# Expert weights loaded two units at a time, eight successive rows per partition, in other buffers

## The reference

```python
def expert_block(args):
    tok, gate, e = args
    hid = xt[tok] @ w1[e] + b1[e]
    out = clamped_swiglu(hid) @ w2[e] + b2[e]
    return out * gate[:, None].astype(out.dtype)
...
y = jnp.zeros((n_tok, D), outs.dtype).at[slot_tok].add(outs.reshape(n_pad, D))
```

## Time and profile before

| | |
|---|---|
| median of 3 runs | 1537.73 us (1536.8 to 1537.91) |
| the profiled execution, its own time | 1541.62 us |
| its span, first to last instruction | 1539.9 us |
| mean granted TensorE clock | 0.983 of full speed |
| PE (TensorE) busy | 93% of the span |
| DVE busy | 63% |
| ACT / POOL busy | 17% / 21% |
| queue q1 (loads issued by SP) | 434.49 MB, 71.7% of 16 engines' span |
| queue q0 (issued by POOL) | 20.31 MB, 5.3% |

### The profile page before, as it was taken

The page is one execution under the profiler, slowest core; times in us unless marked ns, Lnnn a source line. Parts: engine busy times, 40 slices in busy tenths (PEclk is TensorE's granted clock), DMA queues, the critical chain, the costliest instruction groups (busy, mean ns, idle before and its releaser), DMA issues.

```text
span 1539.9 us, 31449 instructions
## 1 busy us (share of the span) xinstructions
PE 1437.1 (93%) x12450; PEld 627.7 (41%) x12450; DVE 963.8 (63%) x1821; ACT 256.4 (17%) x461; POOL 317.3 (21%) x428
## 2 busy tenths in 40 slices
PE   9999999898999999999999999999999999999992
PEld 7777878786552233332222222222222222222220
DVE  5499856642446977576665566666556666655664
ACT  4535243320310010001000000100000010000012
POOL 5633551331230001111111111111111111111100
PEclk9999989999999999999999999999999999999996
DMA  5422100130559999999999999999999999999984
GB/s 177 167 78 80 37 17 6 56 110 1 203 216 394 392 402 402 397 392 402 395 396 387 399 384 394 400 393 390 390 395 389 394 396 391 388 394 388 393 333 132
DMA packets 96785, 456.24 MB, mean 296 GB/s; under 512 B 22978, under 2 KB 36968, under 8 KB 47567
## 3 DMA queue, kind: packets, MB, share of 16 engines
q1 hardware_dynamic: 86974, 434.49, 71.7%
q0 software_dynamic: 9600, 20.31, 5.3%
q10 hardware_dynamic: 144, 0.52, 0.1%
HBM read 442.89 MB, written 20.61 MB: 301 GB/s over the span
## 4 chain that ended last, share of the span: by engine, by line
PE 40%; DMA 33%; DVE 12%; SPq 10%; issue 3%; ACT 2%; POOL 0%; DVEq 0%; POOLq 0%; ACTq 0%
DMA slots<-in_expert_w_dram 32%; PE banks L1709 15%; PE banks L1718 8%; SPq L598 6%; PE banks L1651 3%; SPq L603 3%; PE banks L1439 1%; PE banks L1324 1%; PE banks L1325 1%; PE banks L1326 1%; DVE AR L1947 1%; PE banks L1425 1%; PE banks L1536 1%; PE banks L1504 1%; PE banks L1412 1%
## 5 line engine op out<-in xcount | busy, mean ns | idle before, releaser
L1709 PE MATMUL banks<-slots,BK 128*32 128x512 f32 x6144 | 673.6, 594 | 22.6 <-DMA slots<-in_expert_w_dram 21.6
L1709 PEld LDWEIGHTS banks<-slots,BK 128*32 128x32 f32 x6144 | 195.9, 110 | 490.7 <-issue 368.8
L2228 DVE TENSOR_TENSOR qk<-banks,qk 128x1536 f32<-128x1536 f32 x32 | 56.3, 1758 | 276.2 <-PE banks L1709 275.9
L955 POOL DMA_INDIRECT x_sum<-hT,idy x32 | 46.6, 1457 | 675.7 <-issue 577.0
L1718 PE MATMUL banks<-slots,qk 128*32 128x512 f32 x1536 | 172.5, 594 | 13.2 <-DMA slots<-in_expert_w_dram 13.2
L1718 PE MATMUL banks<-slots,hT 128*32 128x512 f32 x1536 | 171.6, 593 | 13.7 <-DMA slots<-in_expert_w_dram 13.0
L2185 DVE STREAM_TRANSPOSE BK<-AR 32x256 f32<-32x256 f32 x384 | 167.0, 435 | 18.8 <-DMA AR<-h_rows,idx 12.8
L1243 ACT ACTIVATE BK<-qk 128x768 f32<-128x768 f32 x32 | 30.5, 952 | 676.9 <-DVE qk L2228 676.9
L1718 PEld LDWEIGHTS banks<-slots,qk 128*32 128x32 f32 x1536 | 47.7, 109 | 135.1 <-issue 93.6
L1718 PEld LDWEIGHTS banks<-slots,hT 128*32 128x32 f32 x1536 | 47.6, 109 | 134.9 <-issue 93.1
L2195 DVE STREAM_TRANSPOSE qk<-AR 32x192 f32<-32x192 f32 x256 | 94.7, 370 | 3.8
(11 more groups left out here) (380 smaller groups left out, 1446.0 us busy)
## 6 DMA issues: line engine op xcount, KB each, us to landing
slots<-in_expert_w_dram SPq DMA_DIRECT2D x384, 1024.0 KB
slots<-in_w_in_dram SPq DMA_DIRECT2D x13, 1024.0 KB, 5.2
xs<-in_x_dram SPq DMA_DIRECT2D x8, 512.0 KB, 5.1
slots<-in_w_out_dram SPq DMA_DIRECT2D x2, 2048.0 KB, 8.7
x_sum<-slots POOLq DMA_DIRECT2D x1, 2560.0 KB
h_rows<-slots SPq DMA_DIRECT2D x4, 512.0 KB, 7.9
slots<-x_sum SPq DMA_DIRECT2D x4, 512.0 KB, 4.8
out_dram<-hT SPq DMA_DIRECT2D x3, 512.0 KB, 2.6
```

Of the source, the lines that this page charges most:

```text
L1709: ins = nc.tensor.matmul(bank[HID + g][j * CB:(j + 1) * CB, :], xT[q][:, k, g * CB:(g + 1) * CB], raw[n % RAW][:, j, :], start=(k == 0), s ...
L2228: tensor_tensor(inner, hid, bias_row.unsqueeze(1).to_broadcast([P, NG, CW]), ALU.add).then_inc(hid_free, 1)
```

## The change

Two neighbouring units become one DMA of 2 MiB with one semaphore and one wait of SP. Partition p now gets rows 8p to 8p + 7 of w1 and of w2: w1's unit k is row 8p + k on partition p, and a pair of units is one run of 16 KiB per partition, with 64 KiB in DRAM from one partition's run to the next (32 KiB for w2). `turn_x`, `x0` and `turn_act` read every eighth element to match; `turn_act` becomes one instruction in place of 16.

Buffers move. The first area of the ring is now `AR`, free before the output projection; `h2row` moves from area 3 to `qk`; `xg`, `act` and `glu_t` move from `AR` to area 0, `g2row` and `squares` to `BK`. With that, SP begins ten units (all 8 of expert 0, 2 of expert 1) before the output projection, 2 more after its last tile, and none after `x0`. The two first bias loads (L608) move behind the wait for the stores and for `xt_full`. The diff, with unchanged lines cut:

```diff
...
         hrow = region(BKf, 0, 2 * D).rearrange("p (b d) -> p b d", b=2)
-        h2row = region(slot_flat[3], 0, TT * D).rearrange("p (t d) -> p t d", t=TT)
+        h2row = region(qkf, 0, TT * D).rearrange("p (t d) -> p t d", t=TT)
         junk = region(ARf, 0, D)
...
         busy = region(ARf, 3 * D, P)
-        squares = region(ARf, D, D)
-        xg = region(ARf, 0, 2 * D).rearrange("p (b d) -> p b d", b=2)
+        squares = region(BKf, 2 * D, D)
+        xg = region(slot_flat[0], 0, 2 * D).rearrange("p (b d) -> p b d", b=2)
+        last_junk = region(slot_flat[0], 0, D)
         def gated(ap):
             return ap.rearrange("p (g f) -> p g f", g=NG)
-        act, glu_t = (gated(region(ARf, n * D, NG * HC)) for n in (2, 3))
+        act, glu_t = (gated(region(slot_flat[0], n * D, NG * HC)) for n in (2, 3))
         lin_t = gated(region(sbf, 0, NG * HC))
-        g2row = region(ARf, 3 * D, D)
+        g2row = region(BKf, 3 * D, D)
         sig = gated(region(BKf, 0, NG * HC))
...
             return t.rearrange("p (b k) s -> p b k s", b=2)
-        RING = (0, 1, 4, 5, 2, 3)
-        raw = [slots[:, RING[r // 2], r % 2 * 4:r % 2 * 4 + 4, :] for r in range(RAW)]
+        pair_of = [ARf.rearrange("p (k f) -> p k f", k=KT)] + [slots[:, r] for r in (1, 4, 5, 2, 3)]
+        raw = [pair_of[r // 2][:, r % 2 * 4:r % 2 * 4 + 4, :] for r in range(RAW)]
         onehot = region(BKf, 0, TT * TOPK * E).rearrange("p (t k e) -> p t k e", t=TT, e=E)
...
         gatesT = rounded("gatesT", "BK", BW, 2 * CW, [3 * E, T])
-        sum_back = [region(slot_flat[0], n * D, D) for n in range(TT)]
+        sum_back = [region(slot_flat[4], n * D, D) for n in range(TT)]
         slot0, slot1 = (region(sbf, n * TT * NS, TT * NS).rearrange("p (t s) -> p t s", t=TT) for n in range(2))
...
         gfin = region(hTf, 2048, D)
-        outb = [region(hTf, 3072, D), region(hTf, 0, D), region(hTf, D, D), region(ARf, 2 * D, D)]
+        outb = [region(hTf, 3072, D), region(hTf, 0, D), region(hTf, D, D), region(slot_flat[0], D, D)]
         gates_at = region(sbf, NG * HC, NG * 2 * E).rearrange("p (g e) -> p g e", g=NG)
...
         xg_loaded = [sem(f"xg_loaded{q}") for q in range(2)]
-        raw_loaded = [sem(f"raw_loaded{r}") for r in range(RAW)]
+        raw_loaded = [sem(f"raw_loaded{r}") for r in range(RAW // 2)]
         g2_in = sem("g2_in")
...
         def wait_loaded(eng, i, n):
-            eng.wait_ge(raw_loaded[n % RAW], i * (2 * UNITS // RAW * 16) + (n // RAW + 1) * 16)
+            eng.wait_ge(raw_loaded[n % RAW // 2], i * (2 * UNITS // RAW * 16) + (n // RAW + 1) * 16)
         def wait_used(eng, i, n):
...
         block = ctx.enter_context(nc.Block())
-        W1_T = w1[0].rearrange("e (k p) f -> p e k f", p=P)
-        W2_T = w2[0].rearrange("e (j p h) f -> p e j (h f)", p=P, h=2)
+        W1_P = w1[0].rearrange("e (p k) f -> p e k f", p=P)
+        W2_P = w2[0].rearrange("e (p k) f -> p e k f", p=P)
         def load_w1(eng, e, k, n):
-            eng.dma_start(raw[n % RAW].rearrange("p (k c) f -> p k (c f)", k=1),
-                          W1_T[:, bass.ds(e, 1), k:k + 1, :].rearrange("p a k f -> p (a k) f"))\
-               .then_inc(raw_loaded[n % RAW], 16)
+            eng.dma_start(pair_of[n % RAW // 2].rearrange("p k f -> p (k f)"),
+                          W1_P[:, bass.ds(e, 1), k:k + 2, :].rearrange("p a k f -> p (a k f)"))\
+               .then_inc(raw_loaded[n % RAW // 2], 16)
         def load_w2(eng, e, j, n):
-            eng.dma_start(raw[n % RAW].rearrange("p (k c) f -> p k (c f)", k=1),
-                          W2_T[:, bass.ds(e, 1), j:j + 1, :].rearrange("p a k f -> p (a k) f"))\
-               .then_inc(raw_loaded[n % RAW], 16)
+            eng.dma_start(pair_of[n % RAW // 2].rearrange("p k f -> p (k f)"),
+                          W2_P[:, bass.ds(e, 1), 2 * j:2 * j + 4, :].rearrange("p a k f -> p (a k f)"))\
+               .then_inc(raw_loaded[n % RAW // 2], 16)
         def load_bias(eng, e, q):
...
                     sp.dma_start(b2_half[g][n * E:(n + 1) * E], b2[0, :, g * CW:(g + 1) * CW]).then_inc(b2_in, 16)
-            for q in range(2):
-                load_bias(sp, q, q)
             filled(sp, "yT", TT - 1)
             emptied(sp, "Y", TT - 1)
-            for r in range(FIRST):
+            for r in range(FIRST // 2):
                 sp.sem_inc(raw_loaded[r], 16)
-            for k in range(W1U - 2):
+            for k in range(0, W1U, 2):
                 load_w1(sp, 0, k, FIRST + k)
+            for u in (0,):
+                load_w1(sp, 1, u, UNITS + u)
             for tt in range(TT):
...
                 else:
-                    for u in range(FIRST):
+                    for u in (2,):
                         load_w1(sp, 1, u, UNITS + u)
...
             sp.wait_ge(xt_full, 2)
-            for k in range(W1U - 2, W1U):
-                load_w1(sp, 0, k, FIRST + k)
+            for q in range(2):
+                load_bias(sp, q, q)
             def next_units(i, q, e, e_before, begun=0):
-                for u in range(begun, UNITS):
+                for u in range(begun, UNITS, 2):
                     n = q * UNITS + u
-                    wait_used(sp, i, n - RAW)
+                    wait_used(sp, i, n + 1 - RAW)
                     if u == 2:
...
                     next_units(i, q, i * 2 + q, i * 2 + (q - 1))
-            for j in range(W2U):
-                wait_used(sp, E // 2, j - RAW)
+            for j in range(0, W2U, 2):
+                wait_used(sp, E // 2, j + 1 - RAW)
                 load_w2(sp, E - 1, j, j)
...
                         e = sp.value_load(blkexp[0:1, bass.ds(i * 2 + (q - E), 1)], min_val=0, max_val=E - 1)
-                        for u in range(UNITS):
+                        for u in range(0, UNITS, 2):
                             n = W2U + q * UNITS + u
-                            wait_used(sp, i, n - RAW)
+                            wait_used(sp, i, n + 1 - RAW)
                             if u == 2:
...
                 act.wait_ge(sum_added, tt + 1)
-                nc.scalar.activation(junk, xs[:, tt, :], ACT.Square, accum_out=ss[:, tt:tt + 1]).then_inc(act_sq, 1)
+                nc.scalar.activation(last_junk, xs[:, tt, :], ACT.Square, accum_out=ss[:, tt:tt + 1]).then_inc(act_sq, 1)
                 root_mean(tt, 2 * TT + tt + 1, normed)
...
                 for k in range(KT):
-                    ins = nc.tensor.matmul(bank[6 + k // 4][:, (k % 4) * NS:(k % 4 + 1) * NS], h2row[:, tt, k * P:(k + 1) * P],
+                    ins = nc.tensor.matmul(bank[6 + k // 4][:, (k % 4) * NS:(k % 4 + 1) * NS], h2row[:, tt, k::KT],
                                            slot0[:, tt, :], start=(tt == 0 and k % 4 == 0), stop=(tt == TT - 1),
...
                         ins = nc.tensor.matmul(bank[first_bank + g][c * CB:(c + 1) * CB, :],
-                                               actT[q][:, c // 2 * 4 + j, g * CB:(g + 1) * CB],
+                                               actT[q][:, 2 * j + c // 2, g * CB:(g + 1) * CB],
                                                raw[n % RAW][:, c, :], start=(j == 0), stop=(j == W2U - 1))
...
                 for g in range(NG):
-                    rows = xg[g * CB:(g + 1) * CB, q, :].rearrange("p (k a f) -> p a k f", a=4, f=CB)
+                    rows = xg[g * CB:(g + 1) * CB, q, :].rearrange("p (a f k) -> p a k f", a=4, k=KT)
                     for a in range(4):
...
                 dve.wait_ge(act_ready, b + 1)
-                at = actT[q].rearrange("p (h j) (g s) -> p j g h s", h=2, g=NG)
-                for j in range(4):
-                    rows = act[j * CB:(j + 1) * CB].rearrange("p g (a f h) -> p a g h f", a=4, h=2)
-                    for a in range(4):
-                        ins = nc.vector.transpose(at[a * CB:(a + 1) * CB, j], rows[:, a])
-                ins.then_inc(a_ready, 1)
+                nc.vector.transpose(actT[q].rearrange("p m (g s) -> p g m s", g=NG),
+                                    act.rearrange("p g (f m) -> p g m f", m=KT)).then_inc(a_ready, 1)
             def spread_bias(i, b, q):
```

## The result

The changed kernel took 1549.82 us (median of 8 runs, 1543.19 to 1551.87), the kernel before 1537.83 us beside it (8 runs). The ratio is 1.0065 with a 95% interval of 1.0052 to 1.0079: 0.65% slower, where I had forecast 1525 us. Code lines after the edit have one number more than before (w1 is L1710, w2 L1719, `turn_x` L2186); from `turn_act` on they have three fewer (L2192 for L2195, L2225 for L2228).

A forecast was written before the change was run, and what follows sets the result against it. The prediction took DMA, the expert weight stream, as the bound. Its terms, -12.8 - 3 + 1 + 2.5 - 0.7 = -13.0 us, from the 1537.7 us median gave 1524.7, forecast as 1525, with a range of 1505 to 1550.

The forecast's parts named there:

- DMA sets the time: Expert stage: the stream of 374 weight units never pauses; TensorE is not the bound unless the stream gains over 60 us.
- Term 1: Weight stream: 16 KiB runs halve the packets, saving 34 ns per unit over 372 units, -12.8 us.
- The first rival: Weight stream: packet price does not fall (runs cut in two, or one engine's side work sets the pace); 1537.5 us, 14 in 100.
- The upper bound of 54 us: Term 1's most: pauses from gathers, scatters and table loads go by packets and halve, 0.146 us for each of 372 units.
- Term 2: Start of the expert stage: earlier weight units, and less TensorE idling and lower clock before expert 1; 0 to -8, taken -3 us.
- Term 3: Strided reads in `x0`, `turn_x` and `turn_act`: 0 to 8 us before the stream starts, taken +1 us.
- hidden too: `turn_act` on DVE as one instruction, about 0.96 us against 5.9, costs no time except at the end.
- Term 4: End of the stage: TensorE waits for a pair one unit later, +2.5 us once; the last w2's `turn_act` wait goes, -0.7.
- SP's wait per pair costs nothing: Part of Term 4, SP's refilling of the ring: no cost, as ten units are on order behind it.
- Runs apart in DRAM: Rival, weight loads: runs 64 KiB apart (w2: 32 KiB) are slower; at 3%, 27.7 us more, 1552 us; 15 in 100.
- Strided loads at full price: Rival, `x0`'s weight loads before the stream starts: Term 3 is 8 us, total 1532 us; 8 in 100.
- Late side transfers: Rival, gathers behind longer packets: landing perhaps 17 us after issue instead of 8.6, costing only past 30 us; 2 in 100.

The follow-up runs named there:

- experiment 5: Kernel before with light TensorE: third group of rows multiplied only for the first unit of w1 and w2; 1536.11 us.
- experiment 6: Changed kernel with light TensorE: third group of rows multiplied only for the first unit of w1 and w2; 1538.47 us.
- experiment 9: Kernel before with only the lanes of the side rows renamed (place s to lane 6 (s mod 16) + s / 16); 1511.13 us, ratio 0.9834.
- experiment 10: Experiment 1's kernel (16 KiB runs, pairs, contiguous reads) with the lanes of the side rows renamed; 1510.10 us, ratio 0.9809.
- experiment 11: Experiment 3's kernel (8 KiB runs, single units, contiguous reads) with the lanes of the side rows renamed; 1507.49 us, ratio 0.9794.
- experiment 13: Experiment 10's kernel with TensorE's third group of rows multiplied only for the first unit of w1 and w2; 1497.60 us, ratio 0.9726.
- experiment 14: Experiment 13's kernel with every pair moved as two transfers of 8 KiB runs, all waits in pairs kept; 1502.22 us, ratio 0.9753.
- experiment 7: Kernel before with experiment 5's light TensorE, and gathers and scatters of 16 rows in place of 96; 1450.52 us.
- experiment 8: Changed kernel with experiment 6's light TensorE, and gathers and scatters of 16 rows in place of 96; 1444.34 us.
- experiment 4: Kernel before with only the buffers' new homes and ten units ahead; old row order, single units, old `turn_act`; 1534.87 us, ratio 0.9974.
- Experiment 2: Changed kernel with one transfer and semaphore per unit, in 8 KiB runs, strided reads kept; 1544.73 us, ratio 1.0042.
- experiment 1: Changed kernel with `h2row` written permuted by DVE, so `x0` and `turn_x` read contiguously; 1537.03 us, ratio 0.9990.
- experiment 15: Experiment 1's kernel with every pair moved as two transfers of 8 KiB runs, all waits in pairs kept; 1543.92 us, ratio 1.0034.
- experiment 3: Changed kernel with the edits of experiments 1 and 2 together: contiguous reads, single units in 8 KiB runs; 1534.76 us, ratio 0.9969.

## Why the prediction was wrong

The runs are a path of single steps from before to after. Homes and ten units ahead, 0.9974 (-4.0 us); row order with contiguous reads, to 0.9969 (-0.8, inside the intervals); waits in pairs, to 1.0034 (+10.0); runs of 16 KiB, to 0.9990 (-6.8); strided reads, to 1.0065 (+11.5). The sum, +10 us, is the change's own ratio, since each step starts where the last one ended; it is no test of the steps, and each step has an interval of 2 to 3 us either way. The forecast had -13 us. Of the 23 us between the two, the strided reads are 10.5, the waits in pairs 7.5 and the run length 6; the start was 1 us better than forecast.

**The bound.** "DMA sets the time" was right (experiments 5 and 6), but "what counts is when it starts, how long a unit takes, and what follows its end" took the 16 engines as one. Which lanes the side rows stand in is worth 25 to 28 us (9 to 11), by theory X because they load eleven of the engines, and I read a mean share of 1.01 as if it told that all were full.

**Term 1, -12.8, measured -6.8.** The price of a run was right: 32 ns per unit, with few side rows, against 34. The failed step is that it was taken as a plain term for 372 units beside full side rows. The first rival named this ("one engine's side work sets the pace whatever the packets"), but at the price of the whole saving; about half is left. Renamed lanes did not restore it (4 us in experiments 13 and 14), so the rows' spread over the engines does not explain the missing half. The packets' own times show where it goes. From 700 to 1400 us a load packet of 8 KiB takes 311 ns in the median (before) and one of 16 KiB 613 ns (after), as the line said; but the means are 325.5 and 648.9 ns, so that a unit's 64 KiB per engine cost 2604 and 2596 ns, 8 ns less in place of 34. With a quarter of the side rows (7 and 8) the means are 317.0 and 622.7 ns, 45 ns less per unit. The packets during which a side row begins are the long ones: 368 ns in the mean against 318 for the others before, 712 against 624.5 after. So the long packets lose more beside side rows; why they do stays open. The upper bound of 54 us, pauses that shrink with the packets, was never near.

**Term 2, -3, measured -4.0** with single units and contiguous reads (experiment 4). In the change itself it is buried, as term 3 takes the start: the gather of expert 1, issued at 451.81, was in and taken by DVE at 455.99, in 4.2 us where it took 8.62, and PE's idle time before L1691 is 1.89, forecast 1.9. TensorE's clock still fell, but earlier and for longer: it is 0.50 from 444 to 456 us, after passes in which it waited on its weight loads, in place of 0.66 in the mean from 470 to 480. Experiment 2, strided too, shows the same, while experiments 1 and 4 have no such fall between 400 and 1500 us, so this belongs to term 3.

**Term 3, +1, measured +11.5.** The step that failed most. I had both ends, 0 and 8, and chose "near the only row"; but the only row was of the contiguous load and said nothing of the strided one. PEld and DVE by line, of the kernel after, beside the earlier trace rows:

```profile
L1494 PEld LDWEIGHTS banks<-shiftbuf,qk 128*128 128x128 f32 x64 | 15.7, 334 | 0.4 <-issue 0.2
```

```profile
L2186 DVE STREAM_TRANSPOSE BK<-slots 32x256 f32<-32x256 f32 x384 | 246.3, 641 | 7.7 <-DMA slots<-h_rows,idx 1.8 <-DVE pairs_i L2273 0.2
L2192 DVE STREAM_TRANSPOSE hT<-slots 128x768 f32<-128x768 f32 x16 | 25.5, 1593 | 0.6
```

The weight load went from 192 to 334 ns, the pass from 2.00 to 4.10 us, `turn_x` from 435 to 641 ns. The lower clock is not the reason: a pass at clock 1.00 (at 434.5 us) takes 4.1 us of weight loads, one at 0.50 (at 449.9 us) 3.9. In experiment 1 all three are back at 192 ns, 2.00 us and 435 ns. The Trainium skill, "SBUF — State Buffer", section "Door 1: The DMA port swizzle", says that float32 read at a step above four elements pays for a new line each time; these three numbers agree, and weighing it against a row of the other kind of load, I should have taken it. Even the upper bound was short: beyond the passes (7.6 us), `turn_x` is late in the first blocks, where nothing hides it as it does in the earlier trace rows (3.15 us idle before w1 at 515.97, 0.72 in experiment 1). The claim "hidden too" holds in the steady stretch alone. `turn_act` was put at 0.96 us and is 1.59; the step may be the reason, but no run here has that instruction without one. It stays hidden.

**Term 4, +2.5 for the waits, measured +10.0.** "SP's wait per pair costs nothing" is not refuted (1.5 us by itself, inside the intervals); TensorE's wait was put at 2.5 us, "once", and is 5 by itself, 10 with SP's. It is not once: TensorE waits for DMA all through the stage, as the earlier trace rows said with 226 waits. (In experiment 15 the waits are 104, but PE is idle for 48.5 us from 700 to 1400 us, in experiment 3 for 40.0.) The other part, -0.7 for `turn_act` at the end, lies in the row order's -0.8. That a later freed place slows a stream with ten units on order is shown in its size, and how it does so is only argued: the loaded engines' next transfers may come too late after each burst of rows.

**The rivals.** Runs apart in DRAM: no (3 against 4, and 8 against 7 for runs of 16 KiB), nor does the load-only rate tell, 423 GB/s at share 1.00 against 426 at 1.01. The Trainium skill, "DMA: Bandwidth & Descriptors", section "Latency and other measured facts", has a loss for rows 512 KiB apart; at 64 KiB apart no run here shows one. Strided loads at full price: right in kind, put at 8 in 100. Late side transfers: later, but not the 17 us that this rival had. The median from issue to landing of the gathers went from 8.7 to 10.9 us, and a gather's rows last 5.6 us from first to last in place of 3.6; in the steady stretch nothing waits for them. The result lies just inside the range, 1505 to 1550, and that is luck: the top was set for runs apart in DRAM, which cost nothing here, and no rival had the waits in pairs.

The best version found is experiment 11, the homes, ten units ahead, single units, contiguous reads and renamed lanes: 1507.49 us, 2.1% under the kernel before.

## What to carry to other kernels

Where a transfer's rows are dealt to engines, ask which engines get them: a mean share of 1.0 does not show whether some of the 16 are late, and spreading the valid rows over the lanes was worth more than every other edit here. Price a saving on a stream beside the traffic it runs with, since half of a correctly measured packet price was lost. And where an edit brings a strided read onto the path that starts a stage, and the trace has no such read, take the dear end of the bounds, not the row of the contiguous one.

## What the runs showed of the hardware that I had not expected

Renaming the lanes of 96-row indirect transfers so that every six neighbours hold about four valid rows gave 1.7 to 1.8% (ratios 0.9834, and 0.9794 against 0.9969). Three quarters of the side rows gone gave 86 us of 1536, though their queue then moves 7.82 MB in place of 20.31, of 456 in all. A weight load of 128 columns with a step of eight float32 took 334 ns against 192, and the pass of 16 that it paces twice its time. The same 8 KiB loads asked for and awaited two by two, on a ring of twelve units, were 10 us slower.
